# Softmax divisions of two cross-attentions: from one GpSimd multiply per pair of heads to two ScalarE multiplies

## The reference

```
q = (h @ w_q).reshape(b, s, X_HEADS, X_HEAD_DIM) * (X_HEAD_DIM ** -0.5)
kv = mem_n @ w_kv
k = kv[..., :D_MODEL].reshape(b, m, X_HEADS, X_HEAD_DIM)
v = kv[..., D_MODEL:].reshape(b, m, X_HEADS, X_HEAD_DIM)
scores = jnp.einsum('bshd,bmhd->bhsm', q, k).astype(jnp.float32)
p = jax.nn.softmax(scores, axis=-1).astype(v.dtype)
o = jnp.einsum('bhsm,bmhd->bshd', p, v).reshape(b, s, D_MODEL)
return o @ w_o
```

## Time and profile before

| | |
|---|---|
| median of three runs | 1298.67 us (1298.41 to 1298.76) |
| the profiled execution, its own time | 1298.78 us |
| its span | 1297.0 us |
| TensorE clock granted | 0.999 of full speed |
| PE busy | 1277.8 us (99%) |
| DVE busy | 926.0 us (71%) |
| ACT busy | 696.3 us (54%) |
| POOL busy | 133.7 us (10%), 155 instructions |
| line 596 (the divisions) | 8 instructions, 1040 to 2996 ns each |
| first cross-attention, around the change | 760 to 795 us of the span |
| second cross-attention, around the change | 1056 to 1090 us of the span |

### The profile page before, as it was taken

The page is one execution under the profiler, slowest core; times in us unless marked ns, Lnnn a source line. Parts: engine busy times, 40 slices in busy tenths (PEclk is TensorE's granted clock), DMA queues, the critical chain, the costliest instruction groups (busy, mean ns, idle before and its releaser), DMA issues.

```text
span 1297.0 us, 17694 instructions
## 1 busy us (share of the span) xinstructions
PE 1277.8 (99%) x7025; PEld 1095.8 (84%) x7025; DVE 926.0 (71%) x1004; ACT 696.3 (54%) x841; POOL 133.7 (10%) x155
## 2 busy tenths in 40 slices
PE   8999999999999999999999999999999999999997
PEld 6878888888888888888886888888888888988886
DVE  5987765557577865556888684787778675677776
ACT  5664444445754444444557464566666563566664
POOL 3101000001241100000235220000001110000000
PEclk9999999999999999999999999999999999999999
DMA  9823655555532665555651543555557442455540
GB/s 350 303 99 130 204 196 194 194 193 196 204 139 98 209 229 186 186 189 193 236 184 66 194 164 131 201 186 186 191 192 263 175 163 107 157 192 192 184 174 33
DMA packets 36209, 235.49 MB, mean 182 GB/s; under 512 B 4168, under 2 KB 4544, under 8 KB 10160
## 3 DMA queue, kind: packets, MB, share of 16 engines
q1 hardware_dynamic: 30528, 217.07, 47.1%
q0 software_dynamic: 4608, 15.75, 3.7%
q10 hardware_dynamic: 1008, 1.77, 0.4%
HBM read 232.48 MB, written 2.10 MB: 181 GB/s over the span
## 4 chain that ended last, share of the span: by engine, by line
PE 86%; DVE 8%; ACT 3%; issue 1%; POOL 1%; DMA 1%; DVEq 0%; SPq 0%; POOLq 0%; ACTq 0%
PE ps L2146 22%; PE ps L2140 11%; PE ps L2161 7%; PE ps L2163 7%; PE ps L2162 7%; PE ps L1993 4%; PE ps L1995 4%; PE ps L1994 4%; DVE wl L1177 2%; PE ps L2049 2%; PE ps L2051 2%; PE ps L2050 2%; PE ps L2018 1%; PE ps L2020 1%; PE ps L2019 1%
## 5 line engine op out<-in xcount | busy, mean ns | idle before, releaser
L1177 DVE TENSOR_TENSOR wl<-raw,wh 128x2048 fp32r<-128x2048 f32 x203 | 464.8, 2297 | 136.6 <-ACT wh L646 136.3
L646 ACT ACTIVATE wh<-raw 128x2048 fp32r<-128x2048 f32 x203 | 386.9, 1909 | 125.5 <-PE ps L2146 76.7
L2146 PE MATMUL ps<-xhl,wh 128*128 128x512 f32 x1376 | 328.3, 391 | 0.0
L2146 PEld LDWEIGHTS ps<-xhl,wh 128*128 128x128 f32 x1376 | 253.0, 188 | 48.8
L2140 PEld LDWEIGHTS ps<-xhl,wl 128*128 128x128 f32 x1376 | 175.4, 191 | 9.3 <-DVE wl L1177 2.2
L2140 PE MATMUL ps<-xhl,wl 128*128 128x256 f32 x1376 | 179.9, 284 | 2.2 <-DVE wl L1177 1.3
L2161 PE MATMUL ps<-wh,hh 128*128 128x512 f32 x432 | 168.6, 390 | 0.2
L2163 PE MATMUL ps<-wh,hl 128*128 128x512 f32 x432 | 168.2, 389 | 0.0
L2162 PE MATMUL ps<-wl,hh 128*128 128x512 f32 x432 | 168.1, 389 | 0.0
L2161 PEld LDWEIGHTS ps<-wh,hh 128*128 128x128 f32 x432 | 81.1, 188 | 18.4 <-DVE hl L1495 1.1
L2163 PEld LDWEIGHTS ps<-wh,hl 128*128 128x128 f32 x432 | 81.1, 188 | 16.8
(11 more groups left out here) (318 smaller groups left out, 1838.8 us busy)
## 6 DMA issues: line engine op xcount, KB each, us to landing
raw<-in_w_slabs SPq DMA_DIRECT2D x203, 1024.0 KB, 4.8
raw<-in_w_slabs SPq DMA_DIRECT2D x4, 512.0 KB, 8.3
X<-in_x SPq DMA_DIRECT2D x2, 512.0 KB, 5.4
qk<-in_mem POOLq DMA_DIRECT2D x1, 1024.0 KB, 14.6
gains<-in_mem_norm POOLq DMA_DIRECT2D x2, 512.0 KB, 11.0
gains<-in_ln_mix_g POOLq DMA_DIRECT2D x2, 512.0 KB, 12.6
gains<-in_ln_mix_b POOLq DMA_DIRECT2D x2, 512.0 KB, 6.1
gains<-in_ln_ffn_g POOLq DMA_DIRECT2D x2, 512.0 KB, 4.2
```

The lines of the kernel that those rows point to most:

```text
L646: nc.scalar.activation(wh[:, s % RING, :], raw[:, s % LOWS, :], ACT.Copy).then_inc(wh_ready, 1)
L1177: nc.vector.tensor_tensor(wl[:, s % LOWS, :], raw[:, s % LOWS, :], wh[:, s % RING, :].bitcast(F32), ALU.subtract)\
L2146: ins = nc.tensor.matmul(ps[bank + a], wa[:, kt, a * P:(a + 1) * P], xhl[:, kt, :, :], start=False, stop=(kt == KT - 1), skip_group_check= ...
```

## The change

The function `divide_x` moves from GpSimd's program to ScalarE's. On GpSimd it was one multiply of 128x512 per pair; on ScalarE it is two `activation` instructions with the function Copy, one of 128x256 per head, which take the head's reciprocal as a scale with one number per partition. The same semaphores are waited for and raised. On ScalarE the divisions of pairs 0 and 1 stand behind `exps_x(1)` and ahead of `value_hi(1)`, those of pairs 2 and 3 behind `exps_x(3)` and ahead of `heads_hi(0)`.

```
--- before.py
+++ after.py
@@ -588,19 +588,11 @@
             pool.wait_ge(mem_T, 8)
-            def divide_x(l):
-
-                for k, (_, t, j) in enumerate(XA_PAIRS):
-                    p = ar(XA_P, 2, 2, T)[:, k % 2]
-                    pool.wait_ge(x_sums, len(XA_PAIRS) * l + k + 1)
-                    nc.gpsimd.tensor_tensor(p, p, rr[:, t, 2 * j:2 * j + 2].unsqueeze(2).to_broadcast([P, 2, T]), ALU.mult).then_inc(x_norm, 1)
-
...
             gain("pool_norm")
-            divide_x(0)
             norm("ffn0", 1, 1.0 / D, EPS_RMS2)
...
             gain("final_norm")
-            divide_x(1)
             norm("ffn1", 1, 1.0 / D, EPS_RMS2)
@@ -1088,6 +1079,14 @@
                     ins.then_inc(exp_done, 1)
 
+                def divide_x(k):
+                    _, t, j = XA_PAIRS[k]
+                    p = ar(XA_P, 2, 2, T)[:, k % 2]
+                    act.wait_ge(x_sums, len(XA_PAIRS) * l + k + 1)
+                    for u in range(2):
+                        ins = nc.scalar.activation(p[:, u, :], p[:, u, :], ACT.Copy, scale=rr[:, t, 2 * j + u:2 * j + u + 1])
+                    ins.then_inc(x_norm, 1)
+
@@ -1103,6 +1102,8 @@
                 exps_x(0)
                 exps_x(1)
+                divide_x(0)
+                divide_x(1)
                 value_hi(1)
                 queries(3)
                 probs_hi(0)
@@ -1110,6 +1111,8 @@
                 splits(st[f"xo{l}"], 0, 1)
                 exps_x(2)
                 exps_x(3)
+                divide_x(2)
+                divide_x(3)
                 heads_hi(0)
                 probs_hi(2)
                 heads_hi(1)
```

## The result

The changed kernel takes 1300.87 us in the median of 20 runs, beside 1298.69 us for the kernel before on the same chips: +2.18 us. The ratio is 1.0016, 95% interval 1.0010 to 1.0022. Predicted were 1300.8 us and +2.18.

A forecast was written before the change was run, and what follows sets the result against it. TensorE, with 86% of the chain of waits, was taken as the bound. Layer 0's +1.31 and layer 1's +0.87 us make +2.18 on 1298.78, 1300.96; the median 0.11 lower, 1300.8 us; 8-in-10 range 1299.5 to 1302.6.

The forecast's parts named there:

- Price of a multiply: ScalarE, one 128x256 copy with a scale pointer: 501 ns long, 0.41 us of the queue, bounds 0.31 and 0.50.
- First half: Scores, through late `v_hi`, `v_lo` and `q_lo`: head 3 starts 0.59 us later net in layer 0, 0.14 in layer 1.
- Second half: Four multiplies of 0.41 us ahead of head 0's copy: with the first half, `values_x(1)` +1.31 us in layer 0, +0.87 in layer 1.
- The delay passes in full: Behind both places TensorE is busy nearly throughout, so all of the +2.18 us reaches the end.
- Rival 4: Delay taken back later, where TensorE waits for a slab or norm that doesn't shift: 1299.2 us; chance 0.10.
- rival 1: VectorE between `v_hi` and head 3's queries: `v_lo` stays at 1.99 us, 0.77 more per layer, 1302.3 us; chance 0.08.
- rival 5: VectorE: `wl` also gets faster without GpSimd, by 0.77 us; sum 1.28, 1299.9 us; chance 0.05.
- Rival 2: TensorE's clock falls to 1.2 GHz behind the new stops: 5.7 us more, 1306.5 if in one layer; chance 0.04.
- Rival 3: ScalarE's half-idle queue takes the multiplies, only waits for GpSimd go, 0.76 and 0.16 us: 1297.8 us; chance 0.05.
- stop at the projection: TensorE's first projection matmul, held by `xl` of head 0 for over 1 us in both layers.
- stop for `q_lo`: TensorE, layer 0: head 3 waits about 1.4 us for `q_lo`.
- reading of `wl`: VectorE's `wl`, 2.27 us beside GpSimd's multiply, taken as speaking against contention; contention for both would make the sum 1.28 us.

The follow-up runs named there:

- e1: Changed kernel with the divisions of pairs 2 and 3 back on GpSimd, those of 0 and 1 on ScalarE: 1299.36 us, +0.68 over the kernel before.
- e3: Changed kernel with value_hi(1) ahead of divide_x(0) on ScalarE, nothing else: 1300.09 us, +1.41 over the kernel before.
- e2: Changed kernel with the divisions of pairs 0 and 1 back on GpSimd, those of 2 and 3 on ScalarE: 1300.21 us, +1.53 over the kernel before.
- e7: Changed kernel with one 128x512 ScalarE multiply per pair in place of two of 128x256: 1299.89 us, +1.19 over the kernel before.
- e4: Changed kernel with heads_hi(0) ahead of divide_x(2) and divide_x(3), nothing else: 1300.30 us, +1.62 over the kernel before.
- e8: Changed kernel plus two GpSimd multiplies per layer beside VectorE that nobody waits for: 1302.95 us, +4.25 over the kernel before.

## Why the prediction was right

Each step is set against the first transpose, which cancels the kernel's start (769.92 before, 769.48 after; in layer 1 1065.61 and 1066.50).

| step | forecast | measured |
|---|---|---|
| ScalarE's gap ahead of division 1, layer 0 | 0.88 | 0.79 |
| start of `v_hi`, layer 0 | -0.64 | -0.64 |
| start of `q_lo`, layer 0 | +2.31 | +2.29 |
| head 3, layer 0 | +3.06 | +3.04 |
| exponentials of pair 3 | +6.25 | +6.22 |
| head 0's copy | +8.80 | +8.73 |
| first projection matmul | +10.17 | +10.17 |
| `values_x(1)`, layer 0 | +13.03 | +13.02 |
| head 3, layer 1 | +2.44 | +2.44 |
| `values_x(1)`, layer 1 | +12.41 | +12.43 |

- **Price of a multiply.** 0.50 us and 0.40 of the queue were measured (four in 1.70), 0.501 and 0.41 forecast from the rows without and with two pointers.
- **First half.** The chain second reciprocal, division 1, `v_hi`, `v_lo`, `q_lo`, head 3 is shown by e1 (it alone gives +0.57 and +0.15) and by e3 (with `v_hi` ahead it vanishes).
- **Second half.** Shown by e2 (+0.75 and +0.72) and e7 (0.38 us less in each layer with shorter multiplies). That the wait is passed on through head 0's copy is seen in the trace (1.91 us idle on VectorE); e4 shows that the divisions themselves stand close behind as the next limit, which the forecast had not named.
- **The delay passes in full.** Between `values_x(1)` of layer 0 and the first transpose of layer 1 it is 283.97 us before and 284.00 after, and from `values_x(1)` of layer 1 to the end of the span 219.8 us in both. Rival 4 falls.
- **Rivals 1 and 5, `v_lo` and `wl`.** `v_lo` fell to 1.23 us and rises to 1.99 and 1.95 when GpSimd is back (e2, e8): rival 1 falls. `wl` takes 2.27 us with and without GpSimd: rival 5 falls.
- **Rival 2, the clock.** It stays at the 2.4 GHz level, 0.998 of full speed against 0.999 over the span.
- **Rival 3, only gains.** TensorE lost the 0.76 us wait as it says, and got back 1.28 and 0.64 in stops.
- **What was off.** The stop at the projection was announced as over 1 us and is 0.64; part of the time lies in the eight transposes ahead, which take 1.36 us in place of 1.09: division 3 ends at 778.31 (the four multiplies of 1.70 from 776.61), and the fifth transpose starts at 778.36. The forecast left this wait for division 3 out; as it lies ahead of the wait for `xl`, the projection starts where it was forecast all the same. The stop for `q_lo` was to be about 1.4 and is 1.28. Neither moves the sum. The median agrees with the forecast to 0.1 us, which is partly luck: single steps were off by up to 0.09 us, and the price of a multiply, from which most of the sum is made, was a middle between two bounds that by themselves gave +1.04 and +3.26.
- **The reading of `wl`.** The forecast took the 2.27 us of `wl` beside GpSimd as speaking against a contention of the two engines, and priced contention for both instructions at +1.28 us. The last section shows that `wl` pays nothing because it is first, so contention asks for no other sum than the 2.18.

## What to carry to other kernels

Work that is moved to a half-idle engine costs what stands behind it in that engine's queue, not its share of the engine. Before moving, list the instructions right behind the new place, who waits for them and how early they are; here the moved step, with the wait inside it, held back a copy (`v_hi`) that was ready and needed nothing from it. With that copy put ahead, the same step was free in the first half. In a kernel with 99% busy TensorE, single changes of under a microsecond can be told apart in the trace by the distance between two matmuls around the place, though not by the time of whole runs.

## What the runs showed of the hardware that was not expected

GpSimd and VectorE seem to take turns on whole instructions, where VectorE's has two inputs in SBUF, and the one that comes second pays. GpSimd's 128x512 multiply takes 1.04 us alone (the shortest of the eight of line 596). Beside `wl` it takes 3.00: in e8_beside it starts at 766.89, `wl` runs until 768.99, and the multiply ends at 769.89, 0.90 behind that. `wl`, which was there first, loses nothing. The other way round, the second multiply there, of 128x1024, runs until 771.86 in the timeline, 1.89 us long, and `v_lo`, which came during it, ends at 772.94, 1.08 behind; alone it takes 1.2.

The kernel before has the whole chain in layer 0. `wl` ends at 768.35, the first multiply at 769.25 (0.90 behind), `v_lo` at 770.33 (1.08 behind) and the second multiply at 771.23 (0.90 behind). So both of its rows agree with one rule: `wl` was not slowed because it was first, `v_lo` was because it was second. `xl` of head 0, which reads PSUM and one SBUF input, takes its 0.69 us inside GpSimd's fourth multiply, and that keeps its 1.04 us.

The Trainium skill's "GPSIMD Engine Reference", "Key points", has the contention and for both instructions; the forecast took the 2.27 us of `wl` as speaking against it, and should have asked who was first. No run isolates the turn-taking by moving one instruction against the other; what is shown is these ends.
